# Two attention units in one slot of a hand-written order, on one Trainium2 core

## What is computed

```python
q, k, v, gate = split_cols(h @ w_in, ...)      # layer 0: one set; layer 1: three sets q, k, v and one gate
q, k = partial_rope(q, pos), partial_rope(k, pos)
s = (q . k) * SCALE, masked to 0 <= t - s <= max_dist
p = exp(s - m); den = sum(p)                   # layer 0: a sink logit per head joins m and den
o = (p / den) @ v
# layer 0: window 128.  layer 1: (window, dilation) = (128, 1), (512, 4), (2048, 16),
# the three o are merged with weights softmax(m + log(den)) over the three patterns
return o * silu(gate)
```

## Time and profile before

| | us |
|---|---|
| median of three runs | 1458.2 (1453.67 to 1458.45) |
| the profiled execution | 1460.69 |
| its span, first to last instruction | 1458.9 |
| mean granted clock of TensorE | 0.962 of full speed |

### The profile page before, as it was taken

The page is one execution under the profiler, slowest core; times in us unless marked ns, Lnnn a source line. Parts: engine busy times, 40 slices in busy tenths (PEclk is TensorE's granted clock), DMA queues, the critical chain, the costliest instruction groups (busy, mean ns, idle before and its releaser), DMA issues.

```text
span 1458.9 us, 24900 instructions
## 1 busy us (share of the span) xinstructions
PE 1364.8 (94%) x8938; PEld 1230.3 (84%) x8938; DVE 719.7 (49%) x2225; ACT 639.7 (44%) x1769; POOL 398.3 (27%) x443
## 2 busy tenths in 40 slices
PE   4899999998699998999999999999999999997996
PEld 4898988986499987989979889888899799984996
DVE  5543544435732524545435654356644456546625
ACT  6344453536611424445336454346443455446011
POOL 2212141420511011221212823206721218311410
PEclk9999999999599998999999999999999999996898
DMA  5011112122435201011121311202310213215522
GB/s 191 12 30 44 30 53 72 41 77 58 138 102 181 87 22 47 12 36 31 27 65 49 86 52 32 58 23 81 93 27 16 59 49 89 56 35 153 135 101 115
DMA packets 101080, 97.32 MB, mean 67 GB/s; under 512 B 30688, under 2 KB 87520, under 8 KB 100960
## 3 DMA queue, kind: packets, MB, share of 16 engines
q1 hardware_dynamic: 100960, 95.73, 22.2%
HBM read 79.46 MB, written 16.25 MB: 66 GB/s over the span
## 4 chain that ended last, share of the span: by engine, by line
PE 60%; issue 4%; DVE 3%; DMA 3%; ACT 3%; POOL 3%; SPq 1%; DVEq 0%; POOLq 0%; ACTq 0%
PE j_bank L1049 40%; PE s_bank L1151 5%; PE o_bank L1184 5%; PE t_bank L1163 4%; PE t_bank L1130 3%; POOL xr L962 1%; DMA mix_dram<-xr 1%; DMA w_raw<-in_w_out 1%; PE s_bank L1049 1%; PE o_bank L1049 1%; POOL xr L969 1%; ACT probs L1265 1%; DMA ks<-coef_dram 0%; DVE w_lo L1437 0%; ACT gate L1320 0%
## 5 line engine op out<-in xcount | busy, mean ns | idle before, releaser
L1049 PE MATMUL j_bank<-w_hi,ht_hi 128*128 128x384 f32 (+1 forms) x1328 | 455.5, 343 | 15.6 <-DVE ht_lo L1506 7.1
L1049 PE MATMUL j_bank<-w_lo,ht_hi 128*128 128x384 f32 (+1 forms) x1328 | 442.9, 333 | 0.0
L1049 PE MATMUL j_bank<-w_hi,ht_lo 128*128 128x384 f32 (+1 forms) x1328 | 442.3, 333 | 0.0
L1265 ACT ACTIVATE probs<-probs,stat 128x256 f32<-128x256 f32 (+1 forms) x512 | 232.3, 455 | 315.7 <-DVE stat L1469 313.1
L923 POOL TENSOR_TENSOR w_lo<-w_raw,w_hi 128x768 fp32r<-128x768 f32 (+1 forms) x60 | 102.3, 1704 | 717.4 <-ACT w_hi L1256 717.4
L1049 PEld LDWEIGHTS j_bank<-w_hi,ht_hi 128*128 128x128 f32 x1328 | 255.2, 192 | 29.2 <-issue 23.7
L1049 PEld LDWEIGHTS j_bank<-w_lo,ht_hi 128*128 128x128 f32 x1328 | 255.2, 192 | 0.0
L1049 PEld LDWEIGHTS j_bank<-w_hi,ht_lo 128*128 128x128 f32 x1328 | 255.0, 192 | 0.0
L1464 DVE CUSTOM_DVE_ANT_0 probs<-s_bank,masks 128x128 f32<-128x128 f32 (+1 forms) x448 | 141.3, 351 | 77.5 <-PE t_bank L1163 64.9
L1151 PE MATMUL s_bank<-ks,qs 128*128 128x256 f32 (+1 forms) x1024 | 172.4, 292 | 4.2 <-DVE ks L1523 3.3
L1151 PEld LDWEIGHTS s_bank<-ks,qs 128*128 128x128 f32 x1024 | 150.2, 196 | 23.8 <-issue 18.7
(11 more groups left out here) (155 smaller groups left out, 1609.9 us busy)
## 6 DMA issues: line engine op xcount, KB each, us to landing
w_raw<-in_w_qkv SPq DMA_DIRECT2D x64, 384.0 KB, 3.3
coef<-coef_dram SPq DMA_DIRECT2D x96, 128.0 KB, 3.0
w_raw<-in_w_gate SPq DMA_DIRECT2D x32, 256.0 KB, 3.4
mix_dram<-xr SPq DMA_DIRECT2D x12, 512.0 KB, 4.2
w_raw<-in_w_out SPq DMA_DIRECT2D x16, 384.0 KB, 3.5
qk<-mix_dram SPq DMA_DIRECT2D x12, 512.0 KB, 4.3
xr<-in_x SPq DMA_DIRECT2D x8, 512.0 KB, 8.2
out<-xr SPq DMA_DIRECT2D x8, 512.0 KB, 2.7
```

The lines of the kernel that those rows point to most:

```text
L1049: last = pe.matmul(to, a(x_, kt), b(y_, kt), start=(start and kt == kts[0] and x_ == y_), stop=(stop and kt == kts[-1] and x_ == 1))
L1265: last = act.activation(row, row, ACT.Exp, bias=stat[:, s.t % 2, n, r, j:j + 1], scale=SCALE, accum_out=stat[:, s.t % 2, n, r, 2 + j:3 + j])
```

## The change

The loop goes over pairs of slots, `a` and `a + 1`. PE makes both scores, both turns, one piece (`front`), all fills of the two slots, the remaining pieces (`behind`), and the values of the two units that were turned in this pair (`V_BACK` becomes 2). Where `SPLIT_BEHIND` applies and a = 14, `front` is empty and all pieces stand behind the fills. ACT and DVE are rearranged to match: ACT makes the weight splits of both slots, then the even turn's copy, both exps, SiLU, and then the pieces and fills in PE's order, and the work on mixed rows comes last; DVE makes both mask_max, then the odd turn's copy, weight splits, pieces and fills, `store_ot`, and coefficient work last. POOL's and SP's loops stay as they are. The fourth gate piece moves from slot 15 to 14 in layer 1, and `END_COPY` from 12 to 11, which moves `coef_copy` on DVE and `coef_store` and `end_coefs` on SP.

```diff
-            _slots.append((JOBS[-1], [0, 2, 4, 6] if _s.last else [11, 12, 13, 15] if _layer == 1 else [11, 12, 13, 14]))
+            _slots.append((JOBS[-1], [0, 2, 4, 6] if _s.last else [11, 12, 13, 14]))
...
-V_BACK = 3
+V_BACK = 2
...
-END_FIRST, END_EXP, END_LAST, END_TURN, END_COPY = 8, 9, 10, 11, 12
+END_FIRST, END_EXP, END_LAST, END_TURN, END_COPY = 8, 9, 10, 11, 11
...
+def pair_pieces(s, a):
+    pieces = SLOT_PIECES.get((s.t, a), []) + SLOT_PIECES.get((s.t, a + 1), [])
+    first = 0 if s.t in SPLIT_BEHIND and a == UNITS - 2 else 1
+    return pieces[:first], pieces[first:]
+
+def pair_fills(s, a):
+    return fills_at(s, a) + fills_at(s, a + 1)
...
 # PE
-                    for slot in range(UNITS):
-                        score(s, slot)
-                        b, u = unit_before(s, slot, TURN_BACK)
-                        if b:
-                            turn(b, u)
-                        b, u = unit_before(s, slot, V_BACK)
-                        if b:
-                            times_v(b, u)
-                        for key in fills_at(s, slot):
-                            fill(*key)
-                        for key in SLOT_PIECES.get((s.t, slot), []):
-                            piece(key)
+                    for a in range(0, UNITS, 2):
+                        pair = (a, a + 1)
+                        for slot in pair:
+                            score(s, slot)
+                        for b, u in [unit_before(s, slot, TURN_BACK) for slot in pair]:
+                            if b:
+                                turn(b, u)
+                        front, behind = pair_pieces(s, a)
+                        for key in front:
+                            piece(key)
+                        for key in pair_fills(s, a):
+                            fill(*key)
+                        for key in behind:
+                            piece(key)
+                        for b, u in [unit_before(s, slot, V_BACK) for slot in pair]:
+                            if b:
+                                times_v(b, u)
...
 # ACT
+                    for a in range(0, UNITS, 2):
+                        pair = (a, a + 1)
+                        for slot in pair:
+                            w_hi(SLOT_SPLIT.get((s.t, slot), []))
+                        b, u = unit_before(s, a, TURN_BACK)
                         if b:
                             empty_turn(b, u)
+                        for slot in pair:
+                            exps(s, slot)
+                        if SILU_AT in pair and before is not None and before.ends_group:
                             silu(before)
+                        front, behind = pair_pieces(s, a)
+                        for key in front:
+                            empty_piece(key)
+                        for key in pair_fills(s, a):
                             fill_hi(*key)
...
+                        for key in behind:
+                            empty_piece(key)
...
 # DVE
+                    for a in range(0, UNITS, 2):
+                        pair = (a, a + 1)
+                        for slot in pair:
+                            mask_max(s, slot)
+                        b, u = unit_before(s, a + 1, TURN_BACK)
                         if b:
                             empty_turn(b, u)
+                        for slot in pair:
+                            w_lo(SLOT_SPLIT.get((s.t, slot), []))
+                        front, behind = pair_pieces(s, a)
+                        for key in front:
+                            empty_piece(key)
+                        for key in pair_fills(s, a):
                             fill_lo(*key)
...
+                        for key in behind:
                             empty_piece(key)
+                        b, u = unit_before(s, a + 1, V_BACK)
                         if b and u % 4 == 3:
                             store_ot(b, u // NB, (u % NB) // 4)
+                        for slot in pair:
...
```

More of the change, by code:

```diff
@@ L1394, in _ @@
-                        exps(s, slot)
-                        if slot == UNITS - 1:
-                            w_hi(SPLIT_BEHIND.get(s.t, []))
-                        for key in SLOT_PIECES.get((s.t, slot), []):
-                            empty_piece(key)
-                        if slot == (1 if layer == 0 else 3) and before is not None and before.ends_group:
-                            den_exp(before, 0)
-                        if s.last and slot == END_EXP:
-                            den_exp(s, 0)
+                        for slot in pair:
+                            if s.last and slot in SPLIT_MIX:
+                                k = SPLIT_MIX.index(slot)
+                                act.wait_ge(mix_back[k % 3], 16 * (layer * 2 + k // 3 + 1))
+                                mix_split(layer, k, mix_in[k % 3])
+                            if slot == (1 if layer == 0 else 3) and before is not None and before.ends_group:
+                                den_exp(before, 0)
+                            if s.last and slot == END_EXP:
+                                den_exp(s, 0)
@@ L1766, in _ @@
                             fill_lo(*key)
[L1767 removed]
+                        if a == UNITS - 2:
                             w_lo(SPLIT_BEHIND.get(s.t, []))
[L1769 removed]
+                        for key in behind:
                             empty_piece(key)
[L1771 to L1777 removed]
@@ L1789, in _ @@
                         if b and u % 4 == 3:
                             store_ot(b, u // NB, (u % NB) // 4)
+                        for slot in pair:
+                            if before is not None and before.ends_group:
+                                if slot == (1 if layer == 0 else 3):
+                                    coefs_first(before, 0)
+                                if slot == (2 if layer == 0 else 4):
+                                    coefs_last(before, 0)
+                                if slot == LATE_C:
+                                    coef_copy(before, 0)
+                            if s.last and slot == END_FIRST:
+                                coefs_first(s, 0)
+                            if s.last and slot == END_LAST:
+                                coefs_last(s, 0)
+                            if s.last and slot == END_COPY:
+                                coef_copy(s, 0)
+                            if s.last and slot in SPLIT_MIX:
+                                k = SPLIT_MIX.index(slot)
+                                mix_split(layer, k, mix_in[k % 3])
```

60 lines of the change are left out of this document (15 added, 45 removed).

## The result

The changed kernel takes **1549.6 us** (median of 4 runs, 1548.67 to 1551.64), against 1458.28 for the one before (1453.67 to 1458.45): a ratio of 1.0636, 95% interval 1.0613 to 1.066. It is slower by some 91 us, where 61 were forecast; the ratio times 1458.28 is 1551, just over the upper end of the range. The profiled execution took 1549.27 us, with a span of 1547.5 against 1458.9.

The account below looks back on a forecast made before the run. PE's own instruction stream, what it issues and waits for, was taken to bound the kernel. Terms -36 + 26 + 21 + 33 + 6 - 5 - 2 + 18 = +61 on 1458.2 gave 1519 us, range 1478 to 1550.

Parts of the forecast that it names:

- part F: Tails of both layers: table loads saved, mix loads 4 and 5 behind coefficient stores; -5 us, between -15 and +10.
- part G: PE's clock: half of 23 new waits followed by 3.4 us at half speed; +18 us, bounds 0 and +50.
- part A: PE's values: one change of tile shape per pair instead of per unit, 118 x 0.31; -36 us.
- Part B: Score 4 waits for the queries' second-half fill, now behind the front piece, in 12 steps; +26 us.
- Part C: Score 0 waits for the next step's keys, filled in pair (14, 15) behind ACT's w_hi; +21 us.
- Part D: Turn bank: the pair's second turn behind a lone fill waits until that fill is emptied; +33 us, +17 to +40.
- Part E: Pair 14 before by-class steps (t = 6, 9, 12): three fills ahead of the gate piece wait; +6 us.
- Fill on fill: A few present PE waits of one fill on another, 0.23 us in one row, vanish; -2 us.
- Rival 1: Waits come as priced, but the clock holds: 1501 us, chance 0.25.
- rival 2: Every long wait drops the clock, and pair 14 too: 1546 us, chance 0.13.
- Rival 3: Faster: second unit's values ride nearly free, 0.70 us saved per pair, clock held: 1438 us, chance 0.06.
- Rival 5: ACT's block in pair 14 overlaps more (14 less), turn-bank waits 16 less, clock +5: 1476 us, chance 0.10.

Follow-up runs that it names:

- all four edits: Changed kernel with queries' second-half fill ahead of front piece, ACT's fills ahead of emptying it, ACT's odd split behind exps, SP's store behind mix loads 4, 5: 1481.44 us.

## Why the prediction was right in direction and short by 30 us

Of the 28 us between the forecast of 61 and the 88.5 of the profile, part F is 10.5, the waits 7 (about what the gate chain in layer 0 costs), part G 7 and part A 4.

- **Part A** (-36): right in kind, a little large. The loop gives -30 where the forecast's share was -34. With the values alone in twos it gives -33; the entry to V from J, in the changed kernel, is 0.27 us from the last J's start to V's against 0.17 to a fill's, so 0.10 beside the 0.12 that I took over from T. My reason for taking 0.31 in place of 0.36, a cheaper exit into a fill, doesn't hold: in the kernel before, the first product behind the values starts 0.20 us after the last value, be it a score's, a piece's or a fill's. That 0.31 came near was luck in this. The rows for the entry:

```profile
1056.05 0.34 PE L1065 MATMUL j_bank<-w_hi,ht_lo 128*128 128x384 f32 x1
1056.32 1.09 PE L1200 MATMUL o_bank<-probs_t,v 128*64 128x128 f32 x16
...
1063.05 0.34 PE L1065 MATMUL j_bank<-w_hi,ht_lo 128*128 128x384 f32 x1
1063.22 0.60 PE L1146 MATMUL t_bank<-ident,qk 128*128 128x128 f32 x4
```

- **Part B** (+26): right. 12 waits of 2.07 to 2.4 us by the starts; the scores' idle time for `qs` is 25.4 us. Undone alone, it gave back 34, since waits of this kind also bring the clock down.
- **Part C** (+21): right in its chain, slightly large. The idle time for `ks` is 20.2 us, 3.3 of which were there before, so 16.8 in place of 21; single waits are 1.50 to 1.75 us where I had 2.0 to 2.1, and 0.93 to 1.36 in layer 0 where I had 1.4. Undoing ACT's part in it worked in eight steps of eleven.
- **Part D** (+33): right within the loop: 33 us of waits between score and turn and between the two turns, 40 with the one below. That no experiment undid it alone leaves its share of the low clock unknown.
- **Part D's sentence on layer 0** ("layer 0 2.8 in all") is a step that failed. I took ACT to be free when the fill of pair 12 came. It stood at the gate piece, which waits for POOL's mixing; PE was idle for 4.11 and 3.45 us in steps 1 and 2. Of that piece I had only said that moving it costs no product; I did not ask what ACT waits for ahead of emptying it, and by then the fill stood behind it. With the low clock behind the first of them this place was worth 9.5 us, what steps 1 and 2 got back of the 24 by which the profiled execution fell (21 by the medians).
- **Part E** (+6): right in kind, a little large. The idle time ahead of the three fills is 3.6 us a step (0.24, 0.84 and 2.56) where it was 2.2 (1.75 and 0.42), so +4.4 in the three steps.
- **Fill on fill** (-2): didn't come. Four such waits, 1.0 us in all, went, and four of 0.26 us came.
- **Part F** (-5): **the largest failure**, by 10 us with the shares of A and B in these steps. I saw that `END_COPY` puts mix loads 4 and 5 behind the coefficient store, and set it off against table loads and a slide of coef_turn instead of following it: store, six loads, then 6.7 us from 1427.09 until `mix_split` starts, with the last two values behind it. With that order undone, layer 1's stretch from score 0 of the last step on is 175.2 us in place of 180.9, and with all four edits 169.7, 2 under the 171.9 before: about what the forecast had for the two tails. Also, only layer 0 has two SiLUs to bring together; two table loads were saved, not four.
- **Part G** (+18): its rule, half of the long waits, held for the waits that I applied it to: 12 of 23 were followed by a low stretch. But others came behind waits to which I gave none: one at the gate in layer 0, one at the three fills in each of steps 6, 9 and 12 (two of these three had one before), and two at the turns of by-class steps. In the whole run the clock was low in 24 stretches, 11 before. In the loop that made 24.7 us in place of 18. Its basis was thin, too: the kernel before has a fourth long wait, 1.75 us ahead of 953.73, that I left out; a low stretch followed it, which makes three of four. And half of 3.4 us is 1.7, not 1.6, which changes the sum by 1 us.

Rival 1 (the clock holds) and rival 2 (every long wait drops it) fall by that count of 12 in 23, though rival 2's time, 1546, is the nearest to the result, for other reasons than its own. Rival 3 (faster) and rival 4 (no gain from A) fall by the kernel with the values alone in twos: A is 0.29 us a pair, neither 0.70 nor 0. Rival 5 (C half hidden, D low) falls by the waits themselves: 16.8 us for C and 33 for D.

## What to carry to other kernels

Test a grouping with the least that it needs: here the whole gain lay in one loop of PE with the copy that follows it, and each move beside it that a run undid (the fills behind the piece, the split ahead of the exps, the piece emptied ahead of the fills, the store ahead of the loads) had cost time. A piece of work is also the cover of what stands ahead of it, so before a producer is put behind a long block, list who needs its result and how many us of PE's work are left between them. For each wait that moves, follow the engine's list to the next instruction behind it, on SP as well, and price that one; a wait can also cost clock behind it.

## What the runs showed of the hardware

- Behind waits that look alike the clock went either way: 2.00 us ahead of 664.14, then 0.51; 2.32 us ahead of 733.02, then 1.00. Of the 23 waits of B and C, 1.0 to 2.4 us by the starts, 12 were followed by some 3.4 us at the 1.2 GHz level (5 of the 12 in B, 7 of the 11 in C). What decides is open. Taking waits away returned more than their length where they were many: 34 us for 25 of waits, 21 for 12.
- Going from the 128x128 products to the 128x64 ones of the values and back costs some 0.29 us: 112 fewer such excursions took 33 us off the loop in the kernel with the values alone in twos. In the kernel before, a value starts 0.20 us after a turn's last product, where a piece starts 0.03 us after a fill's last product, which has a turn's form. That the shape makes the difference, and not something else in these products (their output in halves of a bank, their own waits), no run shows.
